# A two-model kernel on one core: norm vector signalled apart, first-layer loads reordered, turns and splits moved

## The reference

```python
def first_block(x, p, norm_mix, w_in, ...):
    for i in range(2):                                   # two layers
        h = rmsnorm(x, norm_mix[i])
        z = h @ w_in[i]                                  # 1024 x 5400
        ... = split_cols(z, IN_SPLITS)
        y_a = nsa_mixer(q, kc, vc, ks, vs, kw, vw, gates, ...) @ w_up_nsa[i]   # compressed keys use cmp_w1
        y_b = retention(rq, rk, rv, rg) @ w_up_ret[i]
        x = x + (sigmoid(merge_a) * y_a + sigmoid(merge_b) * y_b) @ w_out[i]
        h = rmsnorm(x, norm_mlp[i])
        x = x + square(relu(h @ w_ff1[i])) @ w_ff2[i]
        gate = sigmoid(rmsnorm(x, norm_ple[i]) @ w_ple_gate[i])
        x = x + gate * (p[i] @ w_ple[i])
    return x

def second_block(x, ...):
    q, k, v, u = split(x @ w_in, ...)                    # sb_ssm_w_in, u is the state-space input
    ...                                                  # stick-breaking attention, SSM, MLP, sparse attention, MLP
```

## Time and profile before

| | |
|---|---|
| median of 3 runs | 1510.5 us |
| the profiled execution, device time | 1510.71 us |
| its span on the core | 1508.8 us |
| TensorE busy | 1456.8 us, 97% |
| VectorE busy | 784.9 us, 52% |
| ScalarE busy | 715.9 us, 47% |
| GpSimd busy | 286.6 us, 19% |
| read from memory | 247.93 MB, 165 GB/s over the span |
| mean granted clock of TensorE | 0.993 |

### The profile page before, as it was taken

One profiled execution on the slowest core, in us unless ns is written; L12 is line 12 of the kernel. 1 busy time (PEld: TensorE's weight loads), 2 busy tenths in 40 slices (PEclk: granted clock), 3 DMA queues, 4 the chain that ended last, 5 costly groups with the idle time before them and its releaser, 6 DMA issues.

```text
span 1508.8 us, 19744 instructions
## 1 busy us (share of the span) xinstructions
PE 1456.8 (97%) x8540; PEld 1221.2 (81%) x8540; DVE 784.9 (52%) x993; ACT 715.9 (47%) x901; POOL 286.6 (19%) x109
## 2 busy tenths in 40 slices
PE   5999999999999999999999999999999999999998
PEld 4787868989867787679899778687989888889986
DVE  3336445544562455355445569885444457554445
ACT  4465425445445463436454436655455326255452
POOL 3689140000026595320000000000000004000000
PEclk9999999999999999999999999999999999999999
DMA  9632435645538432435555373405555453056451
GB/s 352 230 113 91 163 112 188 231 168 198 194 112 290 155 124 87 167 132 215 184 196 195 112 217 112 140 13 204 202 182 208 144 188 120 31 201 237 175 181 70
DMA packets 123142, 250.25 MB, mean 166 GB/s; under 512 B 16960, under 2 KB 28976, under 8 KB 122928
## 3 DMA queue, kind: packets, MB, share of 16 engines
q1 hardware_dynamic: 122792, 248.89, 46.6%
q10 hardware_dynamic: 264, 0.10, 0.0%
HBM read 247.93 MB, written 1.05 MB: 165 GB/s over the span
## 4 chain that ended last, share of the span: by engine, by line
PE 87%; DVE 5%; SPq 3%; ACT 2%; DMA 2%; issue 1%; DVEq 0%; ACTq 0%
PE psum L457 84%; PE psum L464 3%; SPq L2931 2%; DMA ring<-in_w_in 2%; DVE work L1312 1%; DVE x L2445 1%; DVE w_lo L1051 1%; SPq L2956 0%; SPq L2927 0%; DVE rows L1312 0%; ACT w_hi_work L1031 0%; ACT w_hi_tmp L1031 0%; ACT w_hi_rows L1031 0%; DVE ht_hi L1285 0%; DVE tiny L2488 0%
## 5 line engine op out<-in xcount | busy, mean ns | idle before, releaser
L457 PE MATMUL psum<-ht_hi,w_lo 128*128 128x256 f32 x960 | 270.3, 282 | 4.5 <-DVE ht_lo L1312 2.9
L457 PE MATMUL psum<-w_lo,ht_hi 128*128 128x512 f32 (+1 forms) x576 | 225.4, 391 | 0.0
L457 PE MATMUL psum<-w_lo,hid_hi 128*128 128x512 f32 x512 | 202.5, 395 | 0.0
L457 PEld LDWEIGHTS psum<-ht_hi,w_lo 128*128 128x128 f32 x960 | 180.6, 188 | 6.9 <-issue 5.9
L1031 ACT ACTIVATE w_hi_work<-ring 128x2048 fp32r<-128x2048 f32 x43 | 82.3, 1914 | 186.7 <-PE psum L457 170.7
L1051 DVE TENSOR_TENSOR w_lo<-ring,w_hi_work 128x2048 fp32r<-128x2048 f32 x31 | 71.1, 2293 | 137.6 <-ACT w_hi_work L1031 137.6
L457 PEld LDWEIGHTS psum<-w_lo,ht_hi 128*128 128x128 f32 x576 | 109.3, 190 | 21.1 <-issue 1.0
L1121 DVE TENSOR_TENSOR hid_lo<-work,hid_hi 128x512 fp32r<-128x512 f32 x60 | 41.5, 692 | 162.0 <-ACT hid_hi L1099 162.0
L457 PE MATMUL psum<-ht_lo,w_hi_rows 128*128 128x256 f32 x448 | 125.1, 279 | 0.0
L457 PE MATMUL psum<-ht_lo,w_hi_tmp 128*128 128x256 f32 x448 | 125.1, 279 | 0.0
L457 PE MATMUL psum<-ht_hi,w_hi_tmp 128*128 128x256 f32 x448 | 125.0, 279 | 0.0
(11 more groups left out here) (371 smaller groups left out, 3303.4 us busy)
## 6 DMA issues: line engine op xcount, KB each, us to landing
ring<-in_w_ff SPq DMA_DIRECT2D x32, 2048.0 KB, 7.9
ring<-in_mlp_w SPq DMA_DIRECT2D x32, 2048.0 KB, 8.5
ring<-in_w_in SPq DMA_DIRECT2D x20, 2048.0 KB, 8.1
ring<-in_w_out SPq DMA_DIRECT2D x4, 2048.0 KB, 8.1
ring<-in_w_ple_gate SPq DMA_DIRECT2D x4, 2048.0 KB, 8.2
ring<-in_sb_ssm_w_in SPq DMA_DIRECT2D x4, 2048.0 KB, 11.5
ring<-in_dsa_w_in SPq DMA_DIRECT2D x3, 2048.0 KB, 8.1
ring<-in_w_up_nsa SPq DMA_DIRECT2D x2, 2048.0 KB, 7.9
```

What stands on the lines that cost most here:

```text
L457: ins = pe.matmul(o, lhsT, rhs, start=start, stop=stop)
```

## The change

- **Start.** The first small DMA (norm_mix) has a signal of its own, `mix_in`. In the first layer the first turn waits for it alone and turns 8 rows; the other 56 columns of `cols` come from one further matmul behind the turns of x, and a copy on DVE behind its fourth turn.
- **POOL.** Its wait for the constants moves from its first instruction to the rotation in the middle of the layer.
- **Loads.** SP issues in3 ahead of cmp_w1, in both layers. The load of in3 waits for chunk 0.
- **Places.** gate0's upper halves go to tab0 and big instead of work and big. (gate1's stay where they were.)
- **Chunk 8.** The five turns stand later.
- **Output products and ff1.0.** Token turns (`turn_token`) stand inside the fills sooner, and the last of the four stands between two part products of ff1.0. DVE does ff1.0's second lower half after the first two turns.
- **gate0.** Its second lower half is done on DVE after the first two additions of ff2, not ahead of them.
- **Second block.** Part of the first product (tile sb3, first 128 tokens, two of four column groups) stands ahead of the last two turns of x.

```diff
+            "gate0": ("tab0", "big"), "gate1": ("tmp", "rows"),
...
-    small_in = sig("small_in", 16 * 9)
+    small_in = sig("small_in", 16 * 8)
+    mix_in, cols_ready, cols_saved = sig("mix_in", 16), sig("cols_ready"), sig("cols_saved")
...
                     some(0, 0, early)
+                    last_turn()
                     some(1, 0, early)
...
-        pe.wait_ge(small_in.sem, st.at(small_in, 16 * 9))
+        n = 64 if st.where.layer else 8
+        pe.wait_ge(mix_in.sem, st.at(mix_in, 16))
+        if st.where.layer:
+            pe.wait_ge(small_in.sem, st.at(small_in, 16 * 8))
...
-        head.kit.mm(b[:, 0:64], vec_rows, ident[0:64, 0:64], True, True, head.aux.ready)
+        head.kit.mm(b[:, 0:n], vec_rows[0:n], ident[0:n, 0:n], True, True, head.aux.ready)
...
+            pe.wait_ge(small_in.sem, 16 * 8)
+            pe.matmul(scores[:, 0:64], vec_rows, ident[0:64, 0:64], start=True, stop=True).then_inc(cols_ready.sem, 1)
             chunk(0)
...
-        chunk(8, first_token_values, {(0, 1): turn_compressed_probs, (0, 4): lambda: turn_probs(1, 0),
-                                      (0, 6): lambda: turn_probs(1, 1), (1, 1): lambda: turn_probs(1, 2),
-                                      (1, 3): lambda: turn_probs(1, 3)})
+        chunk(8, first_token_values, {(0, 4): turn_compressed_probs, (0, 7): lambda: turn_probs(1, 0),
+                                      (1, 1): lambda: turn_probs(1, 1), (1, 3): lambda: turn_probs(1, 2),
+                                      (1, 5): lambda: turn_probs(1, 3)})
...
-        kit.project(["out0", "out1"], {(0, 1): lambda: turn_mixed(2), (0, 5): lambda: turn_mixed(3), (3, 4): lambda: turn(0)},
+        kit.project(["out0", "out1"], {(0, 1): lambda: turn_mixed(2), (0, 5): lambda: turn_mixed(3), (2, 4): lambda: turn(0, 0),
+                                     (2, 6): lambda: turn(0, 1), (3, 4): lambda: turn(1, 0)},
...
-        turn(1)
+        kit.mlp("", 4, first_token_fed, None, 2, lambda: turn(1, 1))
...
-                lower_split(st, dve, TILES, SPLITS, "ff1.0")
-            if n == 2:
+                lower_half(st, dve, TILES, SPLITS, "ff1.0", 0)
                 gain(0)
                 gain(1)
                 low(0)
                 low(1)
+            if n == 2:
+                lower_half(st, dve, TILES, SPLITS, "ff1.0", 1)
+                gain(2)
+                low(2)
...
-        lower_split(st, dve, TILES, SPLITS, "gate0")
+        lower_half(st, dve, TILES, SPLITS, "gate0", 0)
...
+            if n == 1:
+                lower_half(st, dve, TILES, SPLITS, "gate0", 1)
...
+        state_input(0, slice(0, P))
         head.turn_x(2)
+        state_input(1, slice(0, P))
         head.turn_x(3)
...
-                if n == RING:
+                if n == RING + 1:
                     for kind, j0, nj, place in W1_PARTS:
...
-        pool.wait_ge(const_in.sem, 16)
         for i in range(DEPTH):
```

More of the change, by code:

```diff
@@ L580, in rows_by_split, with mlp @@
             tile_done()
-        def mlp(pre, turns, between=None, second_token=None, between_at=3):
+        def mlp(pre, turns, between=None, second_token=None, between_at=3, last_turn=None):
             def ff1_by_token():
@@ L955, in pe_layer, with turn @@
         tile_done()
-        def turn(t):
-            for half in range(2):
-                kit.turn_token(t, half, out_saved, 2 * t + half + 1)
-        kit.project(["out0", "out1"], {(0, 1): lambda: turn_mixed(2), (0, 5): lambda: turn_mixed(3), (3, 4): lambda: turn(0)},
+        def turn(t, half):
+            kit.turn_token(t, half, out_saved, 2 * t + half + 1)
+        kit.project(["out0", "out1"], {(0, 1): lambda: turn_mixed(2), (0, 5): lambda: turn_mixed(3), (2, 4): lambda: turn(0, 0),
+                                     (2, 6): lambda: turn(0, 1), (3, 4): lambda: turn(1, 0)},
                     aux_.saved, (aux_.nth_save("m1"), aux_.nth_save("m3")))
-        turn(1)
         def turn_fed(n):
@@ L1292, in take_cols @@
         head.dve.wait_ge(head.aux.ready.sem, head.st.at(head.aux.ready, nth))
-        head.dve.tensor_copy(cols, b[:, 0:64]).then_inc(head.st.up(head.aux.saved), 1)
+        n = 64 if head.st.where.layer else 8
+        head.dve.tensor_copy(cols[:, 0:n], b[:, 0:n]).then_inc(head.st.up(head.aux.saved), 1)
         head.dve.wait_ge(head.st.last.sem, head.st.reached())
@@ L1369, in dve_layer @@
             head.turned(3)
+            dve.wait_ge(cols_ready.sem, 1)
+            copy(cols[:, 8:64], scores[:, 8:64]).then_inc(cols_saved.sem, 1)
+            dve.wait_ge(cols_saved.sem, 1)
         else:
@@ L1621, in pool_layer @@
         pool.wait_ge(chunks.saved.sem, st.at(chunks.saved, chunks.nth_save("c4t1")))
+        pool.wait_ge(const_in.sem, 16)
         t4 = [tmp[:, n * 512:(n + 1) * 512].rearrange("p (t h d) -> p t h d", t=TT, d=64) for n in range(4)]
@@ L1878, in ssm_out, with state_input @@
                 mm(o, ca4[:, SJ + j, :], states[:, 1, j, :], False, True, aux_.ready if j % 8 == 7 else None)
+        pe.wait_ge(aux_.saved.sem, st.at(aux_.saved, aux_.nth_save("A.x1")))
+        w = next_tile("sb3", KT, BANK)
+        def state_input(q, tok):
+            for k in range(KT):
+                mm(scores[:, q * S + tok.start:q * S + tok.stop], w[:, k, q * P:(q + 1) * P], hT[:, k, tok], k == 0, k == KT - 1,
+                   u_ready if q == 3 and k == KT - 1 else None)
+        state_input(0, slice(0, P))
         head.turn_x(2)
+        state_input(1, slice(0, P))
         head.turn_x(3)
@@ L1889, in pe_tail @@
         pe.wait_ge(aux_.saved.sem, st.at(aux_.saved, aux_.nth_save("A.x3")))
-        w = next_tile("sb3", KT, BANK)
-        for q in range(4):
-            for k in range(KT):
-                mm(scores[:, q * S:(q + 1) * S], w[:, k, q * P:(q + 1) * P], hT[:, k, :], k == 0, k == KT - 1,
-                   u_ready if q == 3 and k == KT - 1 else None)
+        for q in range(2):
+            state_input(q, slice(P, S))
+        for q in range(2, 4):
+            state_input(q, slice(0, S))
         tile_done()
@@ L2922, in _ @@
             if i:
-                for dst, s in small[:9]:
-                    sp.dma_start(dst, s).then_inc(small_in.sem, 16)
+                for n, (dst, s) in enumerate(small[:9]):
+                    sp.dma_start(dst, s).then_inc((small_in if n else mix_in).sem, 16)
             for n, name in enumerate(TILES):
@@ L2977, in _ @@
         act.wait_ge(small_used.sem, 1)
-        for dst, s in small_loads(0)[:9]:
-            act.dma_start(dst, s).then_inc(small_in.sem, 16)
+        for n, (dst, s) in enumerate(small_loads(0)[:9]):
+            act.dma_start(dst, s).then_inc((small_in if n else mix_in).sem, 16)
         act.wait_ge(eps_set.sem, 4)
```

3 lines of the change are left out of this document (removed).

## The result

The changed kernel is slower, by 0.6%. Its median is 1516.63 us (1511.94 to 1530.69, 15 runs) beside 1508.11 us for the kernel before in the same rounds; the ratio is 1.006 with a 95% interval of 1.004 to 1.008. Forecast were 1502.7 us and "faster" with a chance of 0.87. The profiled execution of the changed kernel is the fastest of its 15: 1511.94 us, span 1510.2 us, mean granted clock 0.994; most of the others took 1515 to 1517 us at 0.988 to 0.992. The profiled execution of before took 1510.71 us.

What follows compares the result with a forecast made beforehand. TensorE, busy for 97% of the span, was taken as the bound, so only ending its waits sooner or less time at its lower clock counts. The terms summed to -7.9 us: about 1502.7 us as a median, range 1496.5 to 1507.5.

Steps and rivals of the forecast that it cites:

- start: Kernel start: TensorE begins at 6.3 to 6.9 us instead of 10.35, chunk 0 at 16.2 to 16.6; -3.7 us.
- loads, layer 1, with clock: Chunk 3's second fill, first layer: TensorE waits for ACT's save behind in4, +3.3 us, and +1.5 for the clock.
- chunk 8: Five later turns find both operands there, so their waits go: -1.6 us a layer, -3.2 in all; bounds 0 and -3.4.
- ff1.0: Behind the output products: earlier turns and splits leave 0.9 us of wait; -2.2 us in both layers, -1.5 for second-layer clock.
- ff2.7: Turns there no longer wait 1.16 us for DVE's additions behind gate0's lower halves: -1.2 us a layer, -2.4 in all.
- second layer's start: With gate0 in tab0, in0 is split sooner and TensorE's wait of 2.03 us goes: -2.0 us.
- loads, layer 2, with clock: Chunk 3, second layer: turns of q 1.0 us sooner, but +1.5 us for a clock that falls at the new wait.
- second block: TensorE waits for sb3, landing about 889.5 us, then one more turn; +1.8 us, bounds -1.8 and +3.
- signs of being right: Earlier first matmul and chunk 0, chunk 8 waits gone, chunk 3 waits, no 3 us cast, DMA wait before sb3's product.
- none of being wrong: No chunk 3 wait, first matmul at 9 to 10 us, over 1 us at chunk 8's values, gate1 holdups of 4 us.
- (c): Rival: norm vector lands late and waits of chunk 8 and ff1.0 come back elsewhere; 1508.7 us, chance 0.09.
- (b): Rival: in4 far later, at C + 33.2 (C: start of chunk 1), makes the kernel 3 us slower, 1513.5 us; chance 0.05.

Runs made afterwards that it cites:

- second profile: The changed kernel run again, nothing altered: median 1516.09 us (11 runs), ratio 1.0045; its profiled execution took 1513.49 us.
- loads only: Kernel before with only cmp_w1 and the small loads issued behind in3: 1516.01 us, ratio 1.0044.
- rest only: Kernel before with only chunk 8's turns, the output products' turns with ff1.0's halves, and gate0's place and halves changed: 1503.82 us, ratio 0.9967.
- one more copy: Kernel before with the first layer's 64-column VectorE copy made in two pieces, 8 and 56 columns: 1511.75 us, ratio 1.0003.
- the loads back: Changed kernel with cmp_w1 and the small loads issued ahead of in3 again: 1515.74 us, ratio 1.0039.
- the pair: The fastest kernel with the state input's products ahead of the second block's turns, against it without: 1498.25 us beside 1493.25.
- the fastest kernel: Changed kernel, load and second-block orders undone, then cmp_w1 loaded in two parts around in3 and out0's slot released early: 1491.7 us, ratio 0.986.
- seven copies more: The fastest kernel with the copy of 56 columns made in 8 pieces, seven VectorE instructions more: 1503.39 us, ratio 0.9897.

## Why the prediction was wrong, step by step

| step | forecast, us | changed, profile | the same, second profile |
|---|---|---|---|
| start | -3.7 | -3.3 | -3.8 |
| loads, layer 1, with clock | +4.8 | +5.5 | +5.5 |
| chunk 8, two layers | -3.2 | -4.1 | -4.1 |
| ff1.0, layer 1 | -1.1 | +0.6 | +0.5 |
| ff1.0, layer 2, with clock | -2.6 | -0.7 | -0.3 |
| ff2.7, two layers | -2.4 | -2.7 | -2.7 |
| second layer's start | -2.0 | -2.2 | -2.2 |
| loads, layer 2, with clock | +0.5 | +1.3 | +1.1 |
| second block | +1.8 | +5.1 | +7.1 |
| last MLP | 0 | +2.0 | +1.9 |
| sum | -7.9 | +1.3 | +2.9 |

Each profile is compared with the one profile of the kernel before, and behind ff2.7 TensorE's own pace is taken. The columns are rounded one by one.

- **Right in mechanism, and about right in size:** the start, the loads of the first layer (the wait of 4.08 us for the save in chunk 3, with the clock at half behind it), chunk 8 (beyond its bound of -3.4), ff2.7, the second layer's start. In all ten profiles with these parts of the change the last two measure the same, -2.7 and -2.2 us. At 442 us there is no cast of 3 us on VectorE, and the wait of 2.03 us of the earlier trace rows is gone.
- **The start is flattered by its baseline.** In the three other profiles with the old order of the small loads (loads only, rest only, one more copy) TensorE starts at 8.98 to 9.22 us, not at 10.35, and in2 is split 0.8 to 1.8 us sooner than in the profile of before. Against these the start gains 1.5 to 2.5 us by the first profile. It makes no difference behind in3: rest only and one more copy are level with before again at in5.
- **All signs of being right came, none of being wrong,** and the kernel is slower. The signs named the places where the change acts. None was named for what stands behind them: ff1.1's load, the start of VectorE's chain, the last MLP.
- **ff1.0 failed at "the fourth quarter goes turn, product, upper half, lower half ... 1.1 us is gained".** That happened, and was worth nothing. The next tile, ff1.1, is loaded only when the output products end, and its splits end at 248.88 us, 0.7 us later than in the kernel before. A gain just ahead of a DMA-bound tile is idle time a little later. I had not followed ff1.1's load; releasing out0's slot one fill sooner is what earned this gain and more.
- **The second block failed as the largest term of the change.** The forecast had TensorE resume at 889.5 us with "one more turn to do (0.5)". It resumed at 886.05, sooner even, but its last two turns (889.27 and 891.50 us) now stand behind 16 and 32 products, most of the first 16 at the low clock, and VectorE's long chain starts only with the last turn. The timeline after:

```profile
886.05 3.38 PE L459 MATMUL psum<-hT,ring 128*128 128x128 f32 x16 [3.89 <-DMA ring<-in_sb_ssm_w_in]
889.27 0.60 PE L466 MATMUL psum<-const,x 128*128 128x128 f32 x4
...
889.91 0.69 DVE L1308 COPY hT<-psum 128x512 f32<-128x512 f32 x1 [5.57 <-PE psum L466]
892.13 0.69 DVE L1308 COPY hT<-psum 128x512 f32<-128x512 f32 x1 [1.53 <-PE psum L466]
892.74 1.77 DVE L2467 TENSOR_SCALAR tmp<-psum 64x256 f32<-64x256 f32 x4
...
958.74 1.46 PE L459 MATMUL psum<-work 64*128 64x256 f32 x13 [2.89 <-DVE tmp L2464]
```

  In the kernel before that chain starts at 891.44:

```profile
889.95 1.52 DVE L1299 COPY hT<-psum 128x512 f32<-128x512 f32 x2
891.44 0.87 DVE L2442 TENSOR_SCALAR tmp<-psum 64x256 f32<-64x256 f32 x2
```

  So VectorE starts 1.3 us later although x was there over 5 us sooner (it is idle for 5.57 us ahead of the first copy), and TensorE, which has less to do by then, waits 2.89 us for the end of the chain. The work moved ahead was work that nobody waited for; what it was moved ahead of was the head of the longest chain. That is 5.1 and 7.1 us instead of 1.8 (7.8 and 5.8 us in the two further profiles with this part, the loads back and the pair's), while the ten profiles without it have -1.6 to +2.7 us there; by the medians of the pair on the fastest kernel it is 5.0 us.
- **The last MLP was no term at all.** Every profile with the norm vector's signal pays 1.9 to 3.6 us there, but for the one with seven copies more (0.0).
- **The spread.** By the ledger the change costs 1.3 and 2.9 us, in the medians 8.5 and 6.3. The profile of before lies 0.9 to 2.6 us above the medians of its later runs (1508.11 to 1509.80), the two profiles of the changed kernel lie 4.7 and 2.6 us under theirs. Most executions of the changed kernel have a mean clock of 0.988 to 0.991, the profiles 0.994 and 0.993; most of the kernel before in the experiments have 0.995 to 0.998, its profile 0.993. A mean of 0.990 beside 0.996 is worth up to 9 us in 1510 (an estimate, were TensorE busy throughout), so the low clock alone could make up for the difference between profiles and medians. The second profile shows one way, a later sb3 and a longer low clock. That the rest is slow stretches too is argued from the mean clock and not shown; no profile of a run of 1517 us was taken.
- **The rivals.** None came as a whole. Of (c), the norm vector was in time, but its second half, that ff1.0's waits come back elsewhere, is what happened. (b) named the place where SP "can issue nothing ahead of in3's wait", but its condition, in4 at C + 33.2, wasn't met (C is 29.9, 3.3 us before that of the earlier trace rows, and 58.2 is C + 28.3). The range allowed one mis-sized term; four terms erred to the same side (ff1.0 twice, second block, last MLP), 8.9 us in all in the first profile.

## What to carry to other kernels

A tuned kernel's start is worth only what the DMA queue behind it allows: put the loads that wait for nothing into the time in which the next one must wait, and look for zeros in the DMA row of the first 40 us. Before work is moved ahead of a turn or a save, ask which chain begins with that turn; and behind each gain name the next tile and when its slot was released. A profile is one execution: the changed kernel's two profiles are the fastest runs of their rounds, so set the medians and the mean clock of all runs beside a profile before its ledger is believed.

## What the runs showed of the hardware

**The lower clock comes by chance behind the same wait.** In the kernel with one more copy TensorE waits 1.48 us at 236.62, as it does in the kernel before (1.47 at 236.67). The clock fell in the first and not in the second:

```profile
236.00:241.00 5.00, 4.38 (x24) 4.41 (x25) 1.16 (x2) 3.11 (x7) 0.00 (x0) 0.66 1.05 391
```

```profile
236.00:241.00 5.00, 4.33 (x37) 4.36 (x38) 1.22 (x2) 3.17 (x7) 0.00 (x0) 1.00 1.04 392
```

This holds for short waits. Behind the 14 waits of 3.3 to 5.4 us that all profiles have behind the start, the clock was low each time; behind the five of 2.8 to 3.1 us it was low once (the wait of 3.05 us in the kernel with the loads alone is one of the four others).

The Trainium skill (TensorE: Matmul & The Clock Gate, section "What's actually happening") says of the slow matmuls at a kernel's start that their number varies from run to run, and that their price is under 1% of a typical kernel's span. Here the low clock also varies in the middle of a kernel; with a change of 0.6% in question, even a price under 1% is too large to leave out.

**VectorE can be shut out for 12 us.** Some executions of most kernels take some 15 us more. Of the kernel before, 15 of the 81 in the three rounds of experiments took 1521 to 1527 us (two others took 1814 and 5138 us, of which nothing more is known). The one with the loads in two parts had none in its first 6 runs and one of the next 6, at 1504.94; with the state input's order on top, none of 6. Two such executions were profiled. In one, seven more copies, VectorE's product took 12.23 us while GpSimd ran lower halves and then a group of eight products:

```profile
116.32 12.23 DVE L1322 TENSOR_TENSOR work<-work,tiny 128x512 f32<-128x512 f32 x1
```

```profile
117.78 4.70 POOL L1060 TENSOR_TENSOR w_lo<-ring,w_hi_scr 128x2048 fp32r<-128x2048 f32 x1
122.33 5.67 POOL L1648 TENSOR_TENSOR tmp<-big,const 128x256 f32<-128x256 f32 x8
```

```profile
141.47 0.88 PE L466 MATMUL psum<-const,work 128*128 128x128 f32 x3 [13.04 <-POOL w_lo L1060]
```

In its base, without the extra copies, the same instruction took 2.06 us:

```profile
116.84 2.06 DVE L1322 TENSOR_TENSOR work<-work,tiny 128x512 f32<-128x512 f32 x1
```

VectorE's product ended only at 128.55 us, 0.55 us behind the end of GpSimd's group of eight (122.33 + 5.67); ScalarE waited for VectorE, its splits came late, GpSimd's next lower halves too, and TensorE stood for 13 us. The other profiled case, the kernel with the loads back, is the same at 552 to 564 us, in layer 2 (12.22 us), with a wait of TensorE of 13.04 us too. The Trainium skill (SBUF — State Buffer, section "Who interferes with whom") says that a VectorE instruction with two inputs in SBUF contends with a GpSimd instruction that reads there. By that rule, the trace agrees; that VectorE can stay shut out past several GpSimd instructions in a row is what these two runs add. Whether the added copies make it likelier (4 of 6 runs against 1 of 12 for the base) was not settled.
